# Grouped values' tile by features with four transposes in the front; chunk gates between state and remainder, and the last chunk by halves, in the delta-rule chain

## The reference

```python
# first block, projections of the normed input h
z = einsum("bsd,de->bse", h, w_in)
q_lat, kv_lat, qb, kb, vb, gate_a, gate_b = split(z)
vb = vb.reshape(B, S, KV_B, HD_B)              # grouped values, 2 heads x 64
ob = blocked_attention(qb, kb, vb)
...
# second block, delta rule, for each chunk
v_new = u_i - einsum("bhcd,bhde->bhce", w_i, state)
o = einsum("bhcd,bhde->bhce", qg, state) + einsum("bhcs,bhse->bhce", a_i, v_new)
state = state * gl[..., None, None] + einsum("bhcd,bhce->bhde", kd, v_new)
...
o = rms_norm(o, out_norm) * silu(z)            # by head, then the output projection
return o.reshape(b_sz, t_len, GDN_V_WIDTH) @ w_out
```

## Time and profile before

| | us |
|---|---|
| median of 3 runs | 2304.18 (2301.99 to 2309.83) |
| the profiled execution | 2309.91 |
| its span from first to last instruction | 2308.1 |
| TensorE busy | 2208.8 |
| DVE busy | 1166.1 |
| ACT busy | 814.3 |

### The profile page before, as it was taken

The page is one execution under the profiler, slowest core; times in us unless marked ns, Lnnn a source line. Parts: engine busy times, 40 slices in busy tenths (PEclk is TensorE's granted clock), DMA queues, the critical chain, the costliest instruction groups (busy, mean ns, idle before and its releaser), DMA issues. The chain is left out here.

```text
span 2308.1 us, 26539 instructions
## 1 busy us (share of the span) xinstructions
PE 2208.8 (96%) x10932; PEld 1748.4 (76%) x10932; DVE 1166.1 (51%) x1696; ACT 814.3 (35%) x1156; POOL 62.6 (3%) x31
## 2 busy tenths in 40 slices
PE   8999999999999999999988999999899998999997
PEld 6877667888888877787876888887686576888885
DVE  5356665542443478778755444412733736444423
ACT  4122672332232264442343322212514733223211
POOL 0001000000000003300000000000000000000000
PEclk9799999999999999999899999999999998999998
DMA  4121003322222222244112222222233021322221
GB/s 174 37 91 55 1 1 103 108 91 91 91 92 96 89 80 88 78 131 101 47 37 73 91 93 99 101 91 91 73 107 113 2 92 55 110 92 91 92 92 54
DMA packets 42969, 190.25 MB, mean 82 GB/s; under 512 B 15504, under 2 KB 16208, under 8 KB 22240
## 3 DMA queue, kind: packets, MB, share of 16 engines
q1 hardware_dynamic: 40512, 184.32, 23.7%
q10 hardware_dynamic: 2336, 4.23, 0.6%
HBM read 184.80 MB, written 3.74 MB: 82 GB/s over the span
## 5 line engine op out<-in xcount | busy, mean ns | idle before, releaser
L421 PE MATMUL psum<-split,weights_high 128*128 128x512 f32 (+1 forms) x1600 | 643.3, 402 | 35.7 <-DVE split L1052 28.8
L240 DVE TENSOR_TENSOR weights_low<-weights_raw,weights_high 128x2048 fp32r<-128x2048 f32 (+1 forms) x155 | 354.1, 2284 | 570.7 <-ACT weights_high L213 570.6
L423 PE MATMUL psum<-split,weights_low 128*128 128x512 f32 (+1 forms) x1600 | 641.0, 401 | 0.0
L422 PE MATMUL psum<-split,weights_high 128*128 128x512 f32 (+1 forms) x1600 | 636.2, 398 | 0.0
L213 ACT CAST weights_high<-weights_raw 128x2048 fp32r<-128x2048 f32 (+1 forms) x164 | 310.1, 1891 | 583.9 <-PE psum L423 576.2
L421 PEld LDWEIGHTS psum<-split,weights_high 128*128 128x128 f32 (+1 forms) x1600 | 303.4, 190 | 115.1 <-issue 22.9
L422 PEld LDWEIGHTS psum<-split,weights_high 128*128 128x128 f32 (+1 forms) x1600 | 303.9, 190 | 76.8 <-issue 1.7
L423 PEld LDWEIGHTS psum<-split,weights_low 128*128 128x128 f32 (+1 forms) x1600 | 303.7, 190 | 72.3
L423 PE MATMUL psum<-hidden,weights_low 128*128 128x512 f32 x352 | 140.4, 399 | 0.0
L422 PE MATMUL psum<-hidden,weights_high 128*128 128x512 f32 x352 | 138.7, 394 | 0.0
L421 PE MATMUL psum<-hidden,weights_high 128*128 128x512 f32 x352 | 138.0, 392 | 0.0
(11 more groups left out here) (422 smaller groups left out, 2752.6 us busy)
## 6 DMA issues: line engine op xcount, KB each, us to landing
weights_raw<-in_weights SPq DMA_DIRECT2D x161, 1024.0 KB, 4.8
minus_c<-minus_c_rows ACTq DMA_DIRECT2D x16, 256.0 KB, 8.3
x_stream<-in_x SPq DMA_DIRECT2D x4, 512.0 KB, 6.9
gdn_in_grown<-gdn_rows SPq DMA_DIRECT2D x4, 512.0 KB, 4.4
chain_grown<-gdn_rows SPq DMA_DIRECT2D x4, 512.0 KB, 4.1
out<-x_stream SPq DMA_DIRECT2D x8, 256.0 KB, 2.1
table<-rope_tables SPq DMA_DIRECT2D x1, 1024.0 KB, 12.3
weights_raw<-in_weights SPq DMA_DIRECT2D x1, 768.0 KB, 4.3
```

The source lines that it names most:

```text
L240: self.nc.vector.tensor_tensor(out=self.low[:, n % 2, 0:width], in0=self.raw[:, n % 2, 0:width], in1=self.high[:, n % 2, 0:width].bitcast( ...
L421: nc.tensor.matmul(bank, wh, ah, start=first, stop=False)
L422: nc.tensor.matmul(bank, wh, al, start=False, stop=False)
L423: return nc.tensor.matmul(bank, wl, ah, start=False, stop=last)
```

## The change

In `front` the grouped values' tile becomes an ordinary `whole_tile` by features. DVE evicts it in one instruction with the factor's tile into `values`, which uses the place of the latent queries' first tile. After the eight latent queries TensorE transposes its four blocks into bank 7, and DVE copies them to `v_b`.

In `GdnChain` DVE's `gate(n-1)` stands directly behind `next_state(n)`, and ACT's `roots(n-1)` directly behind the copies of the new values. For the last chunk TensorE turns chunk 2 ahead of the outputs of chunk 3. These outputs are not copied out of PSUM: ACT squares them from there, and sum, mean, root, reciprocal and gates go half by half (`last_outputs`, `last_gate`), with the outputs read from PSUM. ACT takes the root of chunk 2 ahead of the new values of chunk 3.

```diff
@@ -440,6 +440,7 @@
             table, squares, turned = place("table", 130, [P, 4, T]), place("row_squares_1", 138, [P, 2, T]), place("turned", 142, [P, 2, T])
             factor, latent_ring = place("factor_1", 146, [P, T]), place("latent_ring", 148, [P, 2, T])
             ring = [latent_ring[:, 0, :], latent_ring[:, 1, :], turned[:, 1, :]]
+            values = q_lat[:, 0, :]
             first_q, first_v, first_gate = 10, 18, 22
             n_gates, n_a = 2 * DT, HEADS + 1
             lower, upper = slice(0, HD_B), slice(HD_B, P)
@@ -457,6 +458,7 @@
                 const_in, gains_in, conv_in, table_in = [s.sem(n) for n in ("const_in", "gains_in", "conv_in", "table_in")]
                 x_in = [s.sem(f"x_in_{n}") for n in range(4)]
                 freed, k_read, tanh_ready = s.sem("freed"), s.sem("k_read"), s.sem("tanh_ready")
+                values_turned, values_read = s.sem("values_turned"), s.sem("values_read")
                 (latent_squared, latent_added, latent_summed, latent_mean, latent_root, latent_inverted, latent_spread,
                  latent_scaled, latent_high, latent_low) = [s.sem("latent_" + n) for n in (
                     "squared", "added", "summed", "mean", "root", "inverted", "spread", "scaled", "high", "low")]
@@ -530,6 +532,8 @@
                             pe.wait_ge(head_inverted, 1)
                             if n >= 2:
                                 pe.wait_ge(normed, n - 1)
+                            if n == 1:
+                                pe.wait_ge(values_read, 1)
                             for j in range(TT):
                                 at = (n * TT + j) * 2
                                 for half in range(2):
@@ -577,14 +581,7 @@
                                 latent_spreads()
                         head_sums(0)
                         head_sums(1)
-                        bank = free(9)
-                        high, low = weights.parts(Chunk(c0 + 4), DT)
-                        for j in range(TT):
-                            for k in range(DT):
-                                token = [split[:, n, k, j * P:(j + 1) * P] for n in range(2)]
-                                last = product(psum[:, bank, j * P:(j + 1) * P], token, [high[:, k, P:2 * P], low[:, k, P:2 * P]],
-                                               k == 0, k == DT - 1)
-                        last.then_inc(weights.products, 1)
+                        whole_tile(c0 + 4, 1, free(9), split)
                         head_sums(2)
                         head_sums(3)
                         chunk_ready(latent_chunk)
@@ -596,6 +593,10 @@
                                 last = product(psum[0:DQ_A, bank, :], [y[:, k, h * DQ_A:(h + 1) * DQ_A] for y in parts],
                                                (q_split[:, 0, k, :], q_split[:, 1, k, :]), k == 0, k == 1)
                             last.then_inc(weights.products, 1)
+                        pe.wait_ge(freed, 10)
+                        for j in range(TT):
+                            last = nc.tensor.transpose(psum[:, 7, j * P:(j + 1) * P], values[:, j * P:(j + 1) * P], identity)
+                        last.then_inc(values_turned, 1)
                         head_sums(4)
                         head_sums(5)
                         chunk_ready(latent_chunk + 1)
@@ -758,13 +759,13 @@
                                 last = nc.vector.tensor_tensor(out=qk_b[half, 4 + g, :], in0=psum[rows, 0, :], in1=factor[rows, :], op=ALU.mult)
                         last.then_inc(freed, 1)
                         dve.wait_ge(weights.products, 10)
-                        for j in range(TT):
-                            last = nc.vector.tensor_scalar(v_b[:, j, :], psum[:, 1, j * P:(j + 1) * P], entry.stat[:, 2, j:j + 1], None, ALU.mult)
-                        last.then_inc(freed, 1)
+                        nc.vector.tensor_tensor(out=values, in0=psum[:, 1, :], in1=factor[:], op=ALU.mult).then_inc(freed, 1)
                         low(latent_chunk + 1)
                         for h in range(HEADS):
                             dve.wait_ge(weights.products, first_q + h + 1)
                             nc.vector.tensor_copy(q_a[0:DQ_A, h, :], psum[0:DQ_A, (first_q + h) % 4, :]).then_inc(freed, 1)
+                        dve.wait_ge(values_turned, 1)
+                        nc.vector.tensor_copy(v_b[:], psum[:, 7, :].rearrange("p (j c) -> p j c", j=TT)).then_inc(values_read, 1)
                         dve.wait_ge(head_summed, 6)
                         nc.vector.tensor_scalar(head_stat[:, 0, :], psum[:, 6, 16:16 + 6 * TT * 2], 1.0 / HD_B, EPS,
                                                 ALU.mult, ALU.add).then_inc(head_mean, 1)
@@ -2587,7 +2588,7 @@
                             pe.wait_ge(aq_ready, 2 * n + half + 1)
                             if n >= 1:
                                 pe.wait_ge(qg_ready, n)
-                            b = take(("o", n, half), (o_ready, 2 * n + half + 1))
+                            b = take(("o", n, half), (o_ready, 2 * n + half + 1) if n < TT - 1 else (gated, 2 * n + half + 1))
                             for i, h in enumerate(half_heads[half]):
                                 target = psum[:, b, i * P:(i + 1) * P]
                                 if n >= 1:
@@ -2624,12 +2625,14 @@
                         next_state(n)
                         if more:
                             level6_first(n + 1)
+                        else:
+                            turn(n - 1)
                         outputs(n)
                         if more:
                             key_state(n + 1)
                             level6_second(n + 1)
                             query_key(n + 1)
-                        if n >= 1:
+                        if more and n >= 1:
                             turn(n - 1)
                     turn(TT - 1)
 
@@ -2704,6 +2707,17 @@
                         act.wait_ge(mean, n + 1)
                         nc.scalar.activation(stat[:, 2, n * GH:(n + 1) * GH], stat[:, 1, n * GH:(n + 1) * GH], ACT.Sqrt).then_inc(root, 1)
 
+                    def last_outputs():
+                        n = TT - 1
+                        for half in range(2):
+                            heads = slice(4 * half, 4 * half + 4)
+                            at = slice(n * GH + 4 * half, n * GH + 4 * half + 4)
+                            wait_job(act, ("o", n, half))
+                            act.wait_ge(summed, 2 * n + half - 1)
+                            nc.scalar.activation(squares[:, heads, :], result(("o", n, half)), ACT.Square).then_inc(squared, 1)
+                            act.wait_ge(mean, n + half + 1)
+                            nc.scalar.activation(stat[:, 2, at], stat[:, 1, at], ACT.Sqrt).then_inc(root, 1)
+
                     first_copy(0)
                     second_copy(0)
                     decays(0)
@@ -2711,16 +2725,18 @@
                         more = n + 1 < TT
                         if more:
                             first_copy(n + 1)
+                        if not more:
+                            roots(n - 1)
                         new_values(n)
                         if more:
+                            if n >= 1:
+                                roots(n - 1)
                             second_copy(n + 1)
                             decays(n + 1)
-                        if n >= 1:
-                            roots(n - 1)
-                        outputs(n)
+                            outputs(n)
                         if n >= 1:
                             highs(n - 1)
-                    roots(TT - 1)
+                    last_outputs()
                     highs(TT - 1)
 
                 def vector(dve):
@@ -2826,6 +2842,25 @@
                                                                       in1=z, op0=ALU.mult, op1=ALU.mult)
                             last.then_inc(gated, 1)
 
+                    def last_gate():
+                        n = TT - 1
+                        for half in range(2):
+                            heads = slice(4 * half, 4 * half + 4)
+                            at = slice(n * GH + 4 * half, n * GH + 4 * half + 4)
+                            dve.wait_ge(squared, 2 * n + half + 1)
+                            nc.vector.tensor_reduce(stat[:, 0, at], squares[:, heads, :], AX.X, ALU.add).then_inc(summed, 1)
+                            dve.wait_ge(summed, 2 * n + half + 1)
+                            nc.vector.tensor_scalar(stat[:, 1, at], stat[:, 0, at], 1.0 / P, EPS, ALU.mult, ALU.add).then_inc(mean, 1)
+                            dve.wait_ge(root, n + half + 1)
+                            nc.vector.reciprocal(stat[:, 3, at], stat[:, 2, at]).then_inc(inverted, 1)
+                            dve.wait_ge(inverted, n + half + 1)
+                            for i, h in enumerate(half_heads[half]):
+                                z = z2[:, n, h * P:(h + 1) * P]
```

(13 more changed lines are left out.)

## The result

The changed kernel takes 2291.13 us (median of 7 runs, 2288.97 to 2294.77), the kernel before in the same comparison 2307.15 (7 runs, 2301.99 to 2316.67): a ratio of 0.9925, 95% interval 0.9902 to 0.9947. It is faster by 16 us; the forecast was 23.8 us less than before, at 2280.5 us. None of the 7 runs is that fast, and the median lies above the range of 2274 to 2288. The profiled executions differ by 18.06 us (2309.91 and 2291.85). One later run of the kernel before, 2755.75 us at a mean granted clock of 0.74, stands apart from all others and is left out of what follows.

The account below looks back on a forecast made before the run. TensorE, busy 96% of the span, was taken as the bound, with time to win in its idle gaps and half clock. Front 15.8 plus chain 8.0 gave 23.8 us off the 2304.18 median: forecast 2280.5 us, range 2274 to 2288.

Parts of the forecast that it names:

- Front, 18.30 us removed: Grouped values' tile in front: 96 small products taking 18.30 us become 24 of 512 columns taking 5.7, 12.6 us less.
- Rival (4): Median holds less half clock than the profile, front gains only a few us: no change beyond 0.3% (6.9 us); chance 0.02.
- The span's 5.7 us over the median: Profiled execution of 2309.91 us against the runs' median of 2304.18; the 23.8 us were taken off both.
- The four transposes: Front, added on TensorE: half of the eight transposes that take 1.04 us, costing 0.5 us.
- DVE's copy: Front, 0.7 us added after the last query's copy, expected to be covered by DVE's idle time before the head statistics.
- The sums and the queries: Front, behind the tile: at full clock two-column products take 1.70 us (1.7 gained), latent queries 11.3 us (2.0 gained).
- Chain up to chunk 1's transposes: Gates moved into DVE's idle time end two TensorE waits (3.49, 3.48 us) and speed 16 transposes by 1.7: 8.7 us gained.
- the extra table loads: Chain: ACT's earlier roots make five table loads instead of three, 1.29 us each, expected to delay nobody.
- Chain's end: From chunk 1's transposes to the projection: 15.4 us instead of 15.03, the halves saving nothing in sum, 0.4 us lost.
- The risk that I priced at up to 1.6 us: Half clock in the last outputs after TensorE's mostly idle 4 us before them; chain gain taken as 8.0 instead of 8.3.
- Behind the chain: Stages after the chain: no term in the sum, which held only front 15.8 and chain 8.0 us.
- the isolated gap: Skill's N/2.4 + 2.5 ns: 96 small products 5.4 us, 24 large 5.2, so only the clock would be won; prediction disagreed.

Follow-up runs that it names:

- the chain alone: Only the `GdnChain` edits, front as in the kernel before: 2297.84 us (12 runs), ratio 0.9960; run again, median 2293.92 us (12 runs).

## Why the prediction was wrong

- **Front, 18.30 us removed: the wrong term.** This step failed. The duration came from one profiled execution, in which the clock fell inside the small products, and the prediction took it for the kernel's. With the fall this part of the front goes from 38.34 to 22.36 us, 16.0 against 15.8 forecast. Without it, it goes from 28.63 to 22.36, so 6.3: 5.1 for the products, 1.6 for the short fall in the queries, less 0.4 for the transposes. On three chips 53 of 98 runs of before are at 2305.52 or less, 10 between, 35 from 2312.45. The forecast started from 2304.18, a time of the lower group; no execution of before in that group was profiled, so that it has no long fall is inferred, from the groups and from the chain alone, whose two groups were both profiled. Then 6.3 + 7.8 = 14.1 us is what both parts should give, and 2304.18 less 14.1 is 2290.1; measured were 2291.13 and 2290.91.
- **Rival (4) named the mechanism** (the median holds less half clock than the profile), and I dismissed it because the 96 products are in every run. They are, but their clock isn't. It got 2 in 100, and it had the size wrong too: it said no change beyond 0.3%, and the ratio is 0.9925.
- **The span's 5.7 us over the median** was seen and only carried along. It was a hint: the sum's biggest term was made of half clock. But it was not the size of the fall, which is 9.7 us here (38.34 less 28.63), for that profile was spared other half clock, at the entry of the attention with forgetting.
- **The four transposes** were right: 0.43 against 0.5, and DVE's copy hid as said (0.83 us idle still in front of the head statistics). The sums and the queries were right as well: 1.70 and 11.14 us against 1.7 and 11.3.
- **Chain up to chunk 1's transposes:** 8.7 forecast, 9.2 measured, a mechanism that came out as told. Gates in 2.19 us between state and remainder, the remainder still waits 1.11 us for TensorE, and the extra table loads hold up nobody in this profile (chunk 2's reciprocal follows DVE's other work without a wait at 1147.80). The row's 1.29 us for a switch held; by the 2.66 us of the Trainium skill (ScalarE: Activation LUTs, What ACT_TABLE_LOAD costs) the new values' copies could not have begun at 1147.12.
- **Chain's end:** 15.4 forecast, 16.40 measured, a loss of 1.4 instead of 0.4. The risk that I priced at up to 1.6 us came true: the clock is at 0.60 around the last outputs. In the two runs with chunk 2's transposes behind the outputs the clock falls only after these, and the end is 2.3 to 2.8 us shorter.
- **Behind the chain** the sum assumed no change. Between the two first profiles 4.5 us were lost to half clock, and the second and third profile of before have the fall at the attention's entry as well. That the measured terms of the profile add up to the 23.8 of the forecast is partly luck: the front's 16.0 needs a profile of before with the long fall, and its 0.2 more than forecast stand against 0.2 less in the chain (7.8 instead of 8.0).
- **A rule of the Trainium skill** (TensorE: Matmul & The Clock Gate, Back-to-back issue gap), the isolated gap, gives 56 ns at N = 128, from which I estimated 5.4 us for the 96 products; the section itself says that it under-counts in a stream with weight loads. No run agrees with the 5.4 us: it is 10.67 to 10.75 us at full clock. So the large form wins something at full clock too, 5.1 us.

## What to carry to other kernels

A term that is made of half clock belongs to one execution, not to the kernel: before it goes into a sum, look at the spread of the times and at the granted clock of each run, and price the edit with and without the fall. Where the times stand in two groups with two clocks, a median says which group had more runs: here two medians of the same program differ by 8 us. Compare within a group, and profile an execution of each. The edit of the front takes the upper group away, doubled narrow work takes the lower one away, and the edit of the chain leaves both.

Work that is moved ahead of a product needs its operand as early as the product could start: turning chunk 2 ahead of the last outputs cost 2.3 us. Splitting the chain's end in halves gained nothing.

## What the runs showed of the hardware

- The same 96 products of 128 columns, issued without a gap, keep 2.4 GHz in some executions (10.75 us) and fall to 1.2 GHz in others (18.30 us). With 16 narrow products ahead both happen. With 32 ahead, all seven runs have times of the upper group, and the profiled one is at 0.52 and 0.50. With none directly ahead, none of 24 runs of two kernels has a time of the upper group, and neither profile has the long fall.
- Once the clock was down, the small products didn't bring it back (15.8 us at 0.50, 72.35 to 88.14 in the first profile of before), while products of 512 columns did within 4.5 us.
- Products in the reduced-precision form of float32 (fp32r) at 128 columns, each with a new stationary operand, have a pitch of 0.111 to 0.114 us at full clock and 0.213 at half, against 0.234 at full clock for 512 columns: half the time for a quarter of the work.
- The clock fell after a wait of 3.07 us before the attention with forgetting in the changed kernel (0.54), and not after one of 3.05 us at the same place in the first profile of before (1.00). In 10 of 13 profiles it fell there.
